# Mixture-of-experts layer: experts in order of their counts, with rooms shrinking from 208 to 160 slots and a packed down product

## The chip, the cores and the metric

One core of a Trainium2 chip runs one inference step of a small hybrid diffusion backbone. The metric is the device time of the whole program in microseconds. All arithmetic is float32; products run as pairs of rounded parts ("high" and "low", type fp32r) of both operands.

## The reference, cut to what matters

Two layers run over 640 tokens (128 context, 512 latent) of 1024 features. Layer 0 has a dense channel mixer. Layer 1 has the routed one, which the change concerns:

```python
def moe_swiglu(h, w_router, w_gu, w_down):
    t = h.reshape(B * L, D)
    logits = (t @ w_router).astype(jnp.float32)
    top_v, top_i = lax.top_k(logits, TOP_K)              # 2 of 8 experts
    top_w = jax.nn.softmax(top_v, axis=-1)
    gates = jnp.einsum('nk,nke->ne', top_w, jax.nn.one_hot(top_i, N_EXPERTS, ...))
    gu = jnp.einsum('nd,edf->enf', t, w_gu)              # 1024 -> 2 x 1408
    g, u = jnp.split(gu, 2, axis=-1)
    eo = jnp.einsum('enf,efd->end', jax.nn.silu(g) * u, w_down)   # 1408 -> 1024
    return jnp.einsum('ne,end->nd', gates, eo)
```

The 640 tokens make 1280 token-expert pairs, 160 per expert on average. The kernel computes each expert only on the tokens that chose it. Everything ahead of this layer (modulation, two attention and convolution mixers, the dense mixer) is left alone by the change.

## The kernel before, in words

**Engines and chunks.** Weights stream in chunks of 128 x 1024 float32 (512 KB). SP sends each chunk into one of six raw buffers (`load`, L576; a chunk is sent once the one six before it has been split). ScalarE rounds it to the high part (`split_hi`, L1313-1319), VectorE subtracts to get the low part (`split_lo`, L1864-1867); there are three slots of split weights, so the split of chunk c + 2 stands in the queues of both engines at item c. TensorE waits on `lo_done` for the chunk it needs.

**One list sets the order.** `main_items` (L86) writes out the routed layer: "idx", five "xt", then per expert two "tr", 22 "gu" and 11 "down" items, the next expert's "tr" standing between its predecessor's "gu" and "down". Every engine walks this list in its own `main_expert` (TensorE L1175, ScalarE L1605, VectorE L2431). The last expert's part also has "turn" items and, for VectorE and ScalarE, the mixing of finished rows ("comb", "gate", "join").

**An expert.** Each of the eight experts gets CAP = 208 slots, as a block of 128 and one of 80 (`ROWS`, L28), and they are taken in the order 0 to 7.
- "tr": the gathered token rows `gx` are transposed (L1204) into `hg`, 208 columns of high and 208 of low part for each of eight blocks of features.
- "gu" (`up_chunk`, L1101): for each block, the high weights meet both parts in one matmul of 416 columns (L1108, L1112) and the low weights meet the high part in one of 208 (L1109, L1111). ScalarE and VectorE add the two halves, apply silu and multiply (L1630 to L1652, L2479 to L2492), and split the result into `ea_hi` (L1645, L1652) and `ea_lo` (`lo_part`, L1870-1872).
- "down" (`down_chunk`, L1115): the activations are the stationary side. For each of the two slot blocks there are three products (high-high, low-high, high-low) of two matmuls of 512 columns, 12 matmuls a chunk. ScalarE copies the first block's output to `ey`, VectorE the second's (L2515); POOL's queue writes them to `y_rows` in HBM (`put_rows`, L1777), and gathers the rows of the expert after the next (`fetch_rows`, L1744).
- The last expert's output stays on chip and is scattered by matmuls (L1095, L1149).

**The way in.** VectorE makes the ranks from two counting matmuls (L2289-2298), the selection matrix of expert 0 (`selection(0)`, L2300), the largest count, and from it the flag `most_ready`. TensorE turns the selection into row numbers ("idx", L1195), POOL gathers the rows of expert 0 (L1753). All engines read the largest count and branch: with every count up to 208 they take the path above, else a general path of four rounds over all experts. Meanwhile TensorE transposes the residual stream ("xt", L1171), ScalarE copies it out (L1638), and behind the fifth copy VectorE computes where each token's rows lie (`places`, L2414). SP sends the first six chunks of expert 0 before the route is known (L694); chunks 0 and 1 are split by the last two steps of the output projection ahead (L1494, L2182). Behind the branch it sends the rest (L714-717).

**Later one-time work.** In expert 6's fifth pair, VectorE builds the selection of expert 7 (`selection(LAST_E)`, L2496); POOL then fetches the finished rows of experts 0 to 5 in ten indirect transfers (`fetch_outputs`, L1784), and those of expert 6 later.

## Time and profile before

| | |
|---|---|
| median of 3 runs | 1947.54 us (1946.64 to 1948.92) |
| profiled execution | span 1944.9 us; the page prints no other time for it |
| routed layer, from its first up matmul to the last down matmul | 1234.0 to 1918.7 us of the span |
| TensorE busy | 1889.4 us, 97% |
| VectorE, ScalarE, POOL busy | 1121.2, 799.7, 139.1 us |
| moved | 283.0 MB read, 12.3 MB written |
| granted TensorE clock | 0.992 of full |

The span goes from the first to the last instruction; the timed value has a little around it. A matmul's printed duration includes its pipeline, so two neighbours overlap: what a matmul costs is the distance between starts, or a run of them divided by its count. The same holds, less so, for VectorE and ScalarE.

### The profile page before, as it was taken

To read this page: it belongs to the slowest core of one execution; us is meant where nothing else is said; L and a number is where in the kernel's file an instruction comes from. 1 tells how busy PE (TensorE), PEld (TensorE's weight loads), DVE (VectorE), ACT (ScalarE), POOL (GpSimd) and SP (SyncE) were. 2 spreads that over 40 slices of the span, in tenths; PEclk is the share of its full clock that TensorE was granted. 3 is DMA by queue.
4 is the path that set the end of the run, shared out by engine and by line. 5 is a ranking of instruction groups with operands and counts; after the bars stand their busy time and mean duration, and the time that the engine had idled before them with its cause. 6 is when DMAs were issued, how large, how long until landed. Compare 5 with 4: busy or idle time off the path is not lost.

```text
span 1944.9 us, 30525 instructions
## 1 busy us (share of the span) xinstructions
PE 1889.4 (97%) x12501; PEld 1727.8 (89%) x12501; DVE 1121.2 (58%) x1796; ACT 799.7 (41%) x1334; POOL 139.1 (7%) x109
## 2 busy tenths in 40 slices
PE   8999999999999999999999899899999999999998
PEld 6999768999999999999997597889898988989886
DVE  2643785543433434447347844667676766768576
ACT  4221364322211222232213643556565655656564
POOL 2000000100000000110000012220000000002211
PEclk8999999999999999999999999999999999999999
DMA  9425100334231432304261021678677776768762
GB/s 353 176 90 217 55 1 22 109 112 177 70 120 44 184 120 68 127 25 194 110 194 33 1 68 64 158 232 247 222 247 229 208 240 203 244 203 311 250 197 71
DMA packets 94068, 291.55 MB, mean 150 GB/s; under 512 B 15348, under 2 KB 23924, under 8 KB 93920
## 3 DMA queue, kind: packets, MB, share of 16 engines
q1 hardware_dynamic: 86784, 271.20, 42.5%
q0 software_dynamic: 7136, 18.30, 2.9%
q8 instruction: 102, 1.67, 0.4%
q14 instruction: 46, 0.38, 0.1%
HBM read 283.02 MB, written 12.28 MB: 152 GB/s over the span
## 4 chain that ended last, share of the span: by engine, by line
PE 91%; DVE 5%; ACT 1%; issue 1%; DMA 1%; SPq 0%; POOL 0%; POOLq 0%; ACTq 0%; DVEq 0%
PE ps L740 47%; PE ps L1119 12%; PE ps L1108 12%; PE ps L1109 6%; PE ps L806 2%; PE ps L935 2%; PE ps L881 2%; PE ps L1112 2%; DVE nbias L2020 1%; PE ps L1111 1%; DVE pr L2037 1%; DMA ada_raw<-ada_w 1%; PE ps L1204 1%; ACT pT L1448 0%; PE ps L942 0%
## 5 line engine op out<-in xcount | busy, mean ns | idle before, releaser
L1867 DVE TENSOR_TENSOR w_lo<-raw,w_hi 128x1024 fp32r<-128x1024 f32 x394 | 482.3, 1226 | 386.8 <-ACT w_hi L1319 378.2
L1319 ACT ACTIVATE w_hi<-raw 128x1024 fp32r<-128x1024 f32 x394 | 414.4, 1053 | 343.3 <-PE ps L740 171.1
L1108 PE MATMUL ps<-hg,w_hi 128*128 128x416 f32 x1232 | 379.2, 365 | 1.0 <-DVE hg L2314 0.8
L740 PE MATMUL ps<-a_hi,w_hi 128*128 128x320 f32 x1472 | 341.5, 313 | 3.4 <-DVE a_lo L1898 3.4
L740 PE MATMUL ps<-a_hi,w_lo 128*128 128x320 f32 x1472 | 336.4, 310 | 0.0
L740 PE MATMUL ps<-a_lo,w_hi 128*128 128x320 f32 x1472 | 333.5, 307 | 0.0
L1109 PE MATMUL ps<-hg,w_lo 128*128 128x208 f32 x1232 | 319.2, 259 | 0.0
L740 PEld LDWEIGHTS ps<-a_hi,w_hi 128*128 128x128 f32 x1472 | 247.0, 188 | 12.3 <-issue 8.1
L740 PEld LDWEIGHTS ps<-a_lo,w_hi 128*128 128x128 f32 x1472 | 248.3, 188 | 0.0
L740 PEld LDWEIGHTS ps<-a_hi,w_lo 128*128 128x128 f32 x1472 | 245.0, 188 | 0.0
L1109 PEld LDWEIGHTS ps<-hg,w_lo 128*128 128x128 f32 x1232 | 234.7, 191 | 0.4
L1108 PEld LDWEIGHTS ps<-hg,w_hi 128*128 128x128 f32 x1232 | 232.0, 188 | 3.3 <-DVE hg L2314 1.0
L1915 DVE TENSOR_REDUCE bcol<-ps 128x2 f32<-128x4 f32 x84 | 13.5, 161 | 185.1 <-PE ps L740 185.1
L1119 PE MATMUL ps<-w_hi,ea_hi 128*128 128x512 f32 (+1 forms) x352 | 111.6, 398 | 2.0 <-DVE w_lo L1867 2.0
L1119 PE MATMUL ps<-w_lo,ea_hi 128*128 128x512 f32 (+1 forms) x352 | 110.9, 396 | 0.0
L1119 PE MATMUL ps<-w_hi,ea_lo 128*128 128x512 f32 (+1 forms) x352 | 110.5, 395 | 0.0
L1119 PEld LDWEIGHTS ps<-w_hi,ea_hi 128*128 128x128 f32 (+1 forms) x352 | 58.7, 169 | 24.4 <-DVE w_lo L1867 2.5
L740 PE MATMUL ps<-act_lo,w_hi 128*128 128x320 f32 x352 | 80.3, 309 | 0.0
L740 PE MATMUL ps<-act_hi,w_hi 128*128 128x320 f32 x352 | 80.2, 309 | 0.0
L740 PE MATMUL ps<-act_hi,w_lo 128*128 128x320 f32 x352 | 80.1, 309 | 0.0
L1119 PEld LDWEIGHTS ps<-w_hi,ea_lo 128*128 128x128 f32 (+1 forms) x352 | 59.6, 169 | 22.8 <-issue 0.4
L1119 PEld LDWEIGHTS ps<-w_lo,ea_hi 128*128 128x128 f32 (+1 forms) x352 | 59.3, 168 | 22.5
(285 smaller groups left out, 2452.0 us busy)
## 6 DMA issues: line engine op xcount, KB each, us to landing
raw<-gu_w SPq DMA_DIRECT2D x220, 512.0 KB, 4.4
raw<-moe_down_w SPq DMA_DIRECT2D x88, 512.0 KB, 4.3
ada_raw<-ada_w SPq DMA_DIRECT2D x21, 2048.0 KB, 8.1
raw<-in_w SPq DMA_DIRECT2D x48, 512.0 KB, 9.8
raw<-down_w SPq DMA_DIRECT2D x22, 512.0 KB, 3.5
raw<-out_w SPq DMA_DIRECT2D x16, 512.0 KB, 3.5
ada_pro<-ada_w SPq DMA_DIRECT2D x2, 2048.0 KB, 19.2
y_rows<-ey POOLq DMA_DIRECT2D x7, 512.0 KB, 4.0
```

Source lines behind the costliest of these rows:

```text
L740: ins = nc.tensor.matmul(out[:, hf, 0:c1 - c0], w, o[:, c0:c1], start=f, stop=e)
L806: ins = nc.tensor.matmul(ps[32 * j:32 * (j + 1), g % 4, 0, 0:QCOLS], cs[:, QUAD * q + k, :], src[:, k, j * QCOLS:(j + 1) * QCOLS], start=f ...
L881: ins = nc.tensor.matmul(score_rows(l, m)[:, c0:c1], qT[rows, h, t * P:(t + 1) * P], kT[rows, h, k0 + c0:k0 + c1], start=True, stop=True)
L935: ins = nc.tensor.matmul(outputs(l)[:, i % 2, :], pT[:, i % 2, j * P:(j + 1) * P], vtok[:, k0 // P + j, h * VH:(h + 1) * VH], start=(j == ...
L1108: nc.tensor.matmul(sums, whi, both, start=(k == 0), stop=False)
L1109: nc.tensor.matmul(out, wlo, hg[:, k, 0, :], start=False, stop=False)
L1111: nc.tensor.matmul(out, wlo, hg[:, k, 0, :], start=False, stop=False)
L1112: ins = nc.tensor.matmul(sums, whi, both, start=False, stop=True)
L1119: ins = nc.tensor.matmul(ps[0:ROWS[st_], (g + st_) % 4, hf, :], a[:, k, st_ * P:st_ * P + ROWS[st_]], w[:, n % SPLIT, hf * 512:(hf + 1) * ...
L1204: ins = nc.tensor.transpose(ps[:, slot, k // 2, at:at + ROWS[st_]], gx[0:ROWS[st_], st_, (4 * i + k) * P:(4 * i + k + 1) * P], idn[0:ROWS[ ...
L1319: nc.scalar.activation(w_hi[:, s, :], raw[:, n % RAW, :], ACT.Copy).then_inc(hi_done, 1)
L1867: nc.vector.tensor_tensor(w_lo[:, s, :], raw[:, n % RAW, :], w_hi[:, s, :].bitcast(F32), ALU.subtract)\
```

## The change

Experts are taken in falling order of their counts. The position in that order, not the expert's number, sets the room: 208, 192, 184, 176, 168, 160, 160, 160 slots. The flag that picks the general path now says whether any count exceeds its room.

```diff
+ROOM = [CAP] + [max(160, 200 - 8 * _j) for _j in range(1, EXPERTS)]
+NROWS = [[P, _n - P] for _n in ROOM]
+BASE, LOWER = 64, 256
...
+                    totals = before[:, TT, :]
+                    link(nc.vector.scalar_tensor_tensor(key, totals, float(EXPERTS), iot[:, 0:EXPERTS],
+                                                        op0=ALU.mult, op1=ALU.subtract))
+                    link(nc.vector.tensor_reduce(top, key, AX, ALU.max))
+                    link(nc.vector.tensor_scalar(first, key, top, None, ALU.is_equal))
```

VectorE's order of work at the way in (`column_of` is a multiply and a reduction; `overflow` five and `expert_order` six small operations on 8 or 64 columns):

```diff
-                    selection(0)
+                    column_of(rcol[:], r, first)
+                    select_ranks()
+                    shifted_rows(7, 4)
+                    overflow()
+                    main_expert(MAIN[:1])
+                    expert_order()
                     link(nc.vector.tensor_scalar(rank[:, :, EXPERTS:], rank[:, :, 0:1], float(CAP), None, ALU.subtract))
-                    link(nc.vector.tensor_reduce(most[:], before[:, TT, :], AX, ALU.max))
-                    nc.vector.tensor_copy(most_i[:], most[:]).then_inc(most_ready, 1)
-                    shifted_rows(7, 4)
-                    main_expert(MAIN[:1])
                     weights_of_experts()
```

SP no longer sends chunks ahead of the branch; each source address comes out of a register, and chunk 2 and its followers wait for the gathered rows of the first expert:

```diff
-                    for c in range(PRELOAD):
-                        load(n + c, source(0, c))
...
                     with sp.Else():
-                        for c in range(PRELOAD, MAIN_N):
-                            if c == 2 * UNIT_CH:
-                                load_rows_of_gates()
-                            load(n + c, source(c // UNIT_CH, c % UNIT_CH))
+                        sp.wait_ge(order_ready, 1)
+                        for e in range(EXPERTS):
+                            which = sp.value_load(order_i[0:1, e:e + 1], min_val=0, max_val=EXPERTS - 1)
+                            for cc in range(UNIT_CH):
+                                if (e, cc) == (0, 2):
+
+                                    sp.wait_ge(gx_in, 16 * ST)
+                                if (e, cc) == (2, 0):
+                                    load_rows_of_gates()
+                                load(n + e * UNIT_CH + cc, source_of(which, cc))
```

The splits of chunks 0 and 1 move from the output projection behind the third and fifth stream copy (ScalarE; VectorE likewise), and `places()` moves from behind the fifth to behind the first:

```diff
                 for c in range(OUT_CH):
-                    split_hi(n0 + c + 2, q0 + c)
+                    if l == 0 or c < OUT_CH - 2:
+                        split_hi(n0 + c + 2, q0 + c)
...
+                                if i in (2, 4) and part is MAIN:
+                                    split_hi(n0 + i // 2 - 1, q0)
```

In "tr", "gu" and the activation steps, 208 is replaced by the room of the position (on ScalarE and VectorE too):

```diff
-                                ins = up_chunk(n0 + c, ps[:, slot, 0, 0:CAP], ps[:, slot, 0, 0:2 * CAP])
+                                ins = up_chunk(n0 + c, ps[:, slot, 0, 0:ROOM[e]], ps[:, slot, 0, 0:2 * ROOM[e]],
+                                               gathered_rows(e))
```

From the second position on, the slots above 128 (at most 64) lie with their high part in columns 0 to 63 of one 128-column stationary block and their low part in columns 64 to 127. The first position keeps `down_chunk`.

```diff
+                    def down_lower(n, g, k):
+
+                        for a, w in ((0, w_hi), (1, w_hi), (0, w_lo)):
+                            for hf in range(2):
+                                ins = nc.tensor.matmul(ps[:, g % 4, hf, :], ea[:, k, LOWER * a:LOWER * a + P],
+                                                       w[:, n % SPLIT, hf * 512:(hf + 1) * 512],
+                                                       start=(k == 0 and a == 0 and w is w_hi),
+                                                       stop=(k == FB - 1 and w is w_lo))
+                        return ins
+
+                    def down_upper(n, g, k):
+
+                        for w in (w_hi, w_lo):
+                            for hf in range(2):
+                                ins = nc.tensor.matmul(ps[:, (g + 1) % 4, hf, :], ea[:, k, P:2 * P],
+                                                       w[:, n % SPLIT, hf * 512:(hf + 1) * 512],
+                                                       start=(k == 0 and w is w_hi), stop=(k == FB - 1 and w is w_lo))
+                        return ins
...
+                    def expert_lo(e, f, some, done):
...
+                        nc.vector.tensor_tensor(ea[:, f, P + BASE:BASE + some], full[:, P:some], hi[:, P:some].bitcast(F32),
+                                                ALU.subtract)
+                        nc.vector.tensor_tensor(ea[:, f, LOWER:LOWER + P], full[:, 0:P], hi[:, 0:P].bitcast(F32),
+                                                ALU.subtract).then_inc(alo_done, 1)
...
-                                    nc.vector.tensor_copy(ey[rows, 1, :].rearrange("p (a b) -> p a b", a=2),
-                                                          ps[rows, (g0 + g + 1) % 4]).then_inc(ey_ready, 1)
...
+                                        link(nc.vector.tensor_copy(rest, upper[BASE:BASE + NROWS[e][1]]))
+                                        nc.vector.tensor_tensor(rest, rest, upper[top_rows], ALU.add).then_inc(ey_ready, 1)
```

At the last position, the last chunk's packed product comes first; ScalarE copies its lower half and VectorE adds the other half ahead of `last_outputs`. The last expert's selection and gates are picked out of the tables by its place in the order:

```diff
-                                    selection(LAST_E)
+                                    last_expert()
...
+                    def last_expert():
+
+                        one = perm[:, LAST_E, :]
+                        column_of(glast_f, gates[:], one)
+                        link(nc.vector.tensor_copy(glast[:, :, 0], glast_f))
+                        link(nc.vector.tensor_tensor(glast[:, :, 1], glast_f, glast[:, :, 0].bitcast(F32), ALU.subtract))
+                        column_of(rcol[:], rank[:, :, 0:EXPERTS], one)
+                        select_ranks()
```

The numbers of the slots in `places` use the position instead of the expert (four more small operations).

## Rows read from the trace of the kernel before

**Rows 1.** The page: busy time, share of the span and instructions of each engine.
```profile
PE 1889.4 (97%) x12501; PEld 1727.8 (89%) x12501; DVE 1121.2 (58%) x1796; ACT 799.7 (41%) x1334; POOL 139.1 (7%) x109
```
**Rows 2.** Stretches: length, busy PE, PEld, DVE, ACT, POOL; clock; DMA share; GB/s.
```profile
1319.30:1372.00 52.70, 52.70 (x354) 52.54 (x353) 41.46 (x63) 34.63 (x65) 3.69 (x4) 1.00 0.81 247
...
1785.00:1797.00 12.00, 12.00 (x81) 11.96 (x81) 9.20 (x15) 8.05 (x16) 1.67 (x2) 1.00 0.96 374
```
**Rows 3.** The chain of work that ended last: start us, us, what.
```profile
1144.06 44.19 PE ps L740 x300
...
1288.55 30.66 PE ps L1119 x132
1372.03 1.47 PE ps L1204 x16
...
1711.85 1.47 PE ps L1204 x16
...
1797.20 1.47 PE ps L1204 x16
```
**Rows 4.** Groups of instructions from 1150 us on: busy us, mean ns, idle before.
```profile
L1867 DVE TENSOR_TENSOR w_lo<-raw,w_hi 128x1024 fp32r<-128x1024 f32 x269 | 329.2, 1226 | 174.5 <-ACT w_hi L1319 168.8
...
L2479 DVE TENSOR_TENSOR st<-st,ps 128x208 f32<-128x208 f32 x88 | 32.7, 371 | 18.4 <-ACT st L1630 18.3
...
L2515 DVE COPY ey<-ps 80x1024 f32<-80x1024 f32 x7 | 8.5, 1221 | 2.8 <-PE ps L1119 2.8
```
**Rows 5.** Timeline, TensorE in an up chunk: start us, us, engine, line, operation.
```profile
1256.00 0.37 PE L1108 MATMUL ps<-hg,w_hi 128*128 128x416 f32 x1
...
1256.20 0.26 PE L1109 MATMUL ps<-hg,w_lo 128*128 128x208 f32 x1
...
1256.30 0.37 PE L1108 MATMUL ps<-hg,w_hi 128*128 128x416 f32 x1
```
**Rows 6.** Timeline, weight loads of the two-column matmuls of the "turn" items.
```profile
1844.02 0.64 PEld L1134 LDWEIGHTS ps<-grouped,sel 128*128 128x128 f32 x5
...
1847.55 0.47 PEld L1134 LDWEIGHTS ps<-grouped,sel 128*80 128x80 f32 x5
```
**Rows 7.** Timeline, VectorE in expert 6 just behind the selection of expert 7.
```profile
1773.30 1.23 DVE L1867 TENSOR_TENSOR w_lo<-raw,w_hi 128x1024 fp32r<-128x1024 f32 x1
...
1777.18 1.23 DVE L1867 TENSOR_TENSOR w_lo<-raw,w_hi 128x1024 fp32r<-128x1024 f32 x1
```
**Rows 8.** Timeline, the one-time work of the last two experts; idle time in brackets.
```profile
1769.24 1.27 DVE L2306 TENSOR_SCALAR sel<-iot,rank 128x208 fp32r<-128x208 f32 x5
...
1891.81 1.06 PE L1119 MATMUL ps<-w_hi,ea_hi 128*128 128x512 f32 x2 [2.01 <-DVE w_lo L1867]
...
1918.72 1.41 DVE L2349 SCALAR_TENSOR_TENSOR ey<-ps,gslot,x 128x512 f32<-128x512 f32 x2 [1.14 <-PE ps L1119]
```
**Rows 9.** Timeline, the way into the routed layer, one engine after the other.
```profile
1216.49 1.05 PE L1195 MATMUL ps<-tok,sel 128*128 128x2 f32 x10
...
1215.40 1.27 DVE L2250 SCALAR_TENSOR_TENSOR yab<-ps,rms,pr 128x1024 f32<-128x1024 f32 x1
...
1223.98 2.92 ACT L1638 ACTIVATE x_tok<-ps 128x1024 f32<-128x1024 f32 x3 [4.03 <-issue]
...
1230.85 1.62 ACT L1555 ACTIVATE hg<-ps 128x832 fp32r<-128x832 f32 x2 [1.81 <-PE ps L1204]
...
1221.85 36.97 SPq L581 DMA_DIRECT2D raw<-gu_w  x12
```
**Rows 10.** Loads: the page's landing times, those from 1140 to 1260 us, and issue ns.
```profile
raw<-gu_w SPq DMA_DIRECT2D x220, 512.0 KB, 4.4
...
raw<-gu_w SPq DMA_DIRECT2D x18, 512.0 KB, 8.4
...
L581 SPq DMA_DIRECT2D raw<-gu_w x220: 327/328/3296, 329.6 to 1865.2; - x110
```

More of the change, by code:

```diff
@@ L409, in hybrid_step, with gathered_rows @@
         ht_lo = a_lo[:].rearrange("p a b -> p (a b)").rearrange("p (t d) -> p t d", t=TT)
+        spare = cs[:].rearrange("p k c -> p (k c)")
+        key, first, pos, over = (spare[:, EXPERTS * _i:EXPERTS * (_i + 1)] for _i in range(4))
+        top, glast_f, posit = spare[:, 32:33], spare[:, 40:40 + TT], spare[:, 48:48 + 2 * TT]
+        posit = posit.rearrange("p (t o) -> p t o", o=2)
+        pairs = spare[:, 64:64 + EXPERTS * EXPERTS].rearrange("p (j e) -> p j e", j=EXPERTS)
+        perm = spare[:, 128:128 + EXPERTS * EXPERTS].rearrange("p (j e) -> p j e", j=EXPERTS)
+        picked = spare[:, 192:192 + TT * EXPERTS].rearrange("p (t e) -> p t e", t=TT)
+        ea_two = ea[:].rearrange("p f (a c) -> p f a c", a=2)
+        def gathered_rows(e):
+            return hg[:].rearrange("p k a c -> p (k a c)")[:, 0:KB * 2 * ROOM[e]]\
+                .rearrange("p (k a c) -> p k a c", k=KB, a=2)
         rstd = ss[:].rearrange("p (a b) -> p a b", a=2)
@@ L702, in _ @@
                     sp.wait_ge(most_ready, 1)
-                    with sp.If(sp.value_load(most_i[0:1, 0:1], min_val=0, max_val=T) > CAP):
+                    with sp.If(sp.value_load(most_i[0:1, 0:1], min_val=0, max_val=EXPERTS) > 0):
+                        for c in range(PRELOAD):
+                            load(n + c, source(0, c))
                         load_rows_of_gates()
@@ L1712, in _ @@
                     act.wait_ge(most_ready, 1)
-                    with act.If(act.value_load(most_i[0:1, 0:1], min_val=0, max_val=T) > CAP):
+                    with act.If(act.value_load(most_i[0:1, 0:1], min_val=0, max_val=EXPERTS) > 0):
                         main_expert(MAIN[:len(START)])
+                        for c in range(2):
+                            split_hi(n0 + c, q0)
                         for t in range(TT):
@@ L2309, in selection, with column_of @@
                         ins.then_inc(sel_ready, 1)
-                    def gathered_lo(slot, i, done):
+                    def selection(e, count):
+                        nc.vector.tensor_copy(rcol[:], rank[:, :, e]).then_inc(rcol_set, 1)
+                        dve.wait_ge(rcol_set, count)
+                        select_ranks()
+                    def column_of(dst, table, one):
+                        link(nc.vector.tensor_tensor(picked, table, one.unsqueeze(1).broadcast_to([P, TT, EXPERTS]),
+                                                     ALU.mult))
+                        link(nc.vector.tensor_reduce(dst, picked, AX, ALU.add))
@@ new lines, in overflow @@
+                    def overflow():
+                        link(nc.vector.tensor_tensor(pairs, totals.unsqueeze(1).broadcast_to([P, EXPERTS, EXPERTS]),
+                                                     room[:].unsqueeze(2).broadcast_to([P, EXPERTS, EXPERTS]), ALU.is_gt))
+                        link(nc.vector.tensor_reduce(over, pairs, AX, ALU.add))
+                        link(nc.vector.tensor_tensor(over, over, iot[:, 0:EXPERTS], ALU.subtract))
+                        link(nc.vector.tensor_reduce(most[:], over, AX, ALU.max))
+                        nc.vector.tensor_copy(most_i[:], most[:]).then_inc(most_ready, 1)
```

205 lines of the change are left out of this document (132 added, 73 removed).

## The prediction

> **What bounds the kernel now.** I read the busy table first: TensorE is busy for 97% of the span [rows 1], so only its time, and what it waits for, can move the end. Then the table by stretches: the up phase of one expert (two projections, 22 weight chunks) keeps TensorE at 100% and at the full clock, and the DMA engines at 0.81 [rows 2]. The chain gives the pace: 132 down matmuls in 30.66 us, 232 ns each; the 22 up chunks lie between 1288.55 + 30.66 = 1319.21 and 1372.03, which is 52.8 us or 2.40 us a chunk, eight pairs of 300 ns; 300 matmuls of 320 columns elsewhere take 147 ns each [rows 3]. One expert takes (1711.85 - 1372.03) / 4 = 84.95 us, eight of them some 680 [rows 3]. Of the side engines VectorE is nearest: 1.23 us for each chunk's low part, and four operations of 0.37 us for each pair of chunks [rows 4].
>
> **How much a pair shrinks.** A pair is a "high" matmul of 2 x 208 columns and a "low" one of 208, starting 0.20 and 0.10 us apart [rows 5]. From 320 to 512 columns the time grows by (232 - 147) / 192 = 0.443 ns a column [rows 3]; on that line 416 columns cost 190 ns and 208 cost 98, together 288, while the pair takes 300. So with 190 for the high one, the low one takes 110. Its neighbour shows why: during the low matmul the 128-column weights of the next high one are loaded. Where matmuls have only two moving columns, such loads follow each other by (0.64 - 0.19) / 4 = 112 ns with 128 weight columns and by (0.47 - 0.15) / 4 = 80 ns with 80 [rows 6]. I read the low matmul as waiting for that load already. Fewer slots then shorten the high matmul alone: 2 x 0.443 = 0.89 ns a slot and pair.
> Two rules of the Trainium skill pull apart here, both on the page TensorE: Matmul & The Clock Gate. The section "Wait — 56ns, not 53.3ns?" has warm matmuls start N / 2.4 + 2.5 ns apart; by it alone the low matmul would fall from 89 to 69 ns and the up phases would give 60 us. The section "LDWEIGHTS (loading the stationary operand)" has a load of P columns take P / 1.2 ns, 107 for 128, which forbids just that. The 112 ns of the bare loads side with the second.
>
> **The sum: gains.** Rooms are 208, 192, 184, 176, 168, 160, 160, 160: 256 slots fewer over eight experts. Up: 176 pairs an expert x 256 x 0.89 ns = 40 us. Down: for the seven experts behind the first, 12 matmuls a chunk become 10 (six for the slots under 128, four for the packed block): 7 x 11 x 2 = 154 x 232 ns = 36 us. The transposes of the gathered rows (1.47 us for 16 [rows 3]) lose at most 0.3 us each expert; I take none. Gains 76 us.
>
> **What the side engines do then.** A pair of chunks in a room of 160 lasts 2 x 8 x (300 - 48 x 0.89) = 4.12 us on TensorE. VectorE, when it is behind and waits for nobody, needs 3.88 us for its share of such a pair at 208 slots (its chunk splits at 1773.30 and 1777.18) [rows 7]. Narrower operations take off 4 x 48 x (1226 - 371) / 816 = 0.2 us [rows 4]; the packed low part is two operations for one, bounded by nothing and another 0.37, taken as 0.1. So 3.8 against 4.1: it stays covered, but its spare time per pair falls from 0.9 us to 0.3. ScalarE's share shrinks and adds nothing in the loop. Where VectorE gets extra work, TensorE now waits sooner:
> - Each expert's output of the packed block is a copy and an add instead of one copy of 1.22 us [rows 4]: VectorE reaches the third chunk's split 1.2 us later, about 2 x 1.22 + 1.23 + links = 3.9 us into the up phase, where that chunk is due at 4.1. Covered; 0.
> - Expert position 6 (the last but one) builds the last one's selection inside its up phase: 1.27 us for five compares [rows 8] and six operations on single columns, under 0.2 us each; TensorE waited (1797.20 - 1711.85) - 84.95 = 0.4 us for these [rows 3]. Six more of 0.2 us come, and the lead over TensorE shrinks by two chunk times of 0.34. I take 2 us more, between 1 and 3.5.
> - The last expert's up phase has three row mixings of 1.2 us each on VectorE; the pair then asks 3.8 + 1.2 = 5.0 against 4.12: 3 x 0.9 less a lead of about 1.3, 1.3 us. Behind it TensorE waited 2.01 us for a split whose chain (last product, table load, mixing, split) does not depend on it [rows 8]; the two down chunks that cover it are 4 x 232 ns shorter: 0.9 us more.
> - At the end, VectorE waited 1.14 us for the last down matmul before it scaled the outputs [rows 8]. The last three down chunks are now 3 x 0.46 = 1.4 us shorter, and the add of the packed block (1.2 us) is put before the scaling: -1.14 + 1.4 + 1.2 = 1.5 us on the tail.
> Together 5.7 us.
>
> **The start of the routed layer.** Before, six chunks were loaded and two split long before the route was known, under the output projection; the new order of experts is known only behind the counts. VectorE now does, ahead of the branch flag (till now written just before the row shift that starts at 1215.40 [rows 9]), three operations for the largest expert, two for its column, five for the overflow test, and the row shift of 1.3 us that stood behind it: 10 x 0.2 + 1.3 = 3.3 less one rank operation of 0.2, so the flag comes at about 1218.5. The index matmuls start at 1216.49 behind filler matmuls of TensorE's own [rows 9], so the 1.0 us ahead of the selection is hidden there; without the fillers it would be on the path. The index results are read about 0.8 us later; six operations for the order (1.3 us) stand ahead of the gate weights that ScalarE waits for before it branches, so its first stream copy moves from 1223.98 to about 1226.2. Behind its third and fifth copies it now makes two splits (2 x 1.05 us), where before the gathered rows arrived last; places() moves behind the first copy and is off the path. Sum: 2.2 + 2.1, less the 1.8 that ScalarE idled for the gathered rows at 1230.85 [rows 9]: 2.5 us. SP issued its first chunk after the branch at 1221.85 [rows 9]; with the flag 3.2 us later but only 1.5 us behind its own last store before, that becomes about 1223.5, plus reading the order; loads land in 4.4 us [rows 10], at best at 1228, at worst (8.4 us, the median of the loads in this stretch [rows 10]) after 1232, where ScalarE wants them at 1229.5. The third chunk is sent behind the gathered rows and has two chunks' time left. I take 3 us, between 2 and 8. The two splits taken out of the projection stood beside its matmuls and give nothing back.
>
> **Loads.** Every weight load gets a source address out of a register, and SP reads one number per expert. No row shows such a load; the nearest are 0.33 us median and 3.3 us at most per issue [rows 10]. SP needs one per 2.07 us in the shortest rooms and runs up to five chunks ahead: I take 0. The data: 512 KB per 2.07 us is 253 GB/s beside row traffic, where stretches that are full moved 374 [rows 2]. Only the early fetch of finished rows fills the engines; it may delay weights by 0 to 4 us; I take 0.5.
>
> **Sum:** 40 + 36 - 5.7 - 3 - 0.5 = 67 us off the profiled span of 1944.9, which gives 1878. The page prints no other time for that execution; the median of the runs, 1947.5, is 2.6 above the span, and 67 off it is 1880.5; I say 1881. The sum's own bounds: gains 74 to 78, costs 5 to 20, so 1873 to 1893.
>
> **Rivals.**
> - *The low matmul shrinks too* (12%). For it: the pair's 300 ns differ from the line's 288 by 12 only. Against: 112 ns between bare loads. Then 176 x 256 x 0.443 = 20 us more: 1861, less where VectorE (3.8) then bounds the pairs of the short rooms (3.84), so about 1863. It is the outcome of the first of the two rules of the Trainium skill named above (TensorE: Matmul & The Clock Gate).
> - *Weights come late* (14%): the chunks are requested at the same lead of six buffers but used 16% faster; full stretches stood at a share of 0.96 already [rows 2]. If the fetches and the start each cost what they can, 4 + 5 us, and the small stalls come at their upper bounds, 1893 or a few more.
> - *SP becomes the bound, and the kernel slower* (2%): a load with a register address would have to cost SP over 84.9 / 33 = 2.57 us; at the longest issue of the trace, 3.3 us, 231 loads give 231 x 0.73 = 168 us more than now, 2115. The median of 0.33 speaks against it.
> - *The shrunk path is not taken* (under 1%): where counts exceed rooms, all engines take the general path of four rounds, well over a millisecond slower. The reference's routing of the given inputs has the sorted counts 205, 179, 176, 150, 148, 148, 138, 136; all fit.
> My forecast has the other 71%. The range of 8 in 10, 1864 to 1895, takes in the first rival's upper part, the bounds above and most of the second. A measurement of this kernel tells 0.2% (4 us) from no change: faster 0.97, same 0.01, slower 0.02.
>
> **What the profile after would show.** The high matmuls of short rooms 147 ns and the low ones still 0.10 to 0.11 us apart, the last rooms' up phase 45.5 us; if it is 42.5, the first rival holds. Ten matmuls a down chunk, 2.32 us. VectorE without "idle" before its splits in the short rooms, yet no TensorE wait beside those named. The first up matmul near 1237. A wait of TensorE on w_lo that goes back to raw and DMA would show the second rival; SP issues longer than 2 us the third.

## The result, and the profile after

| | before | after |
|---|---|---|
| median | 1947.09 us (1944.95 to 1948.92, 4 runs) | 1916.29 us (1912.51 to 1921.1, 4 runs) |
| profiled execution | span 1944.9 us | 1912.51 us, span 1910.7 us |
| granted TensorE clock | 0.992 | 0.985 |

The ratio is 0.9842, with a 95% interval from 0.9828 to 0.9857. The change gains 31 us where 67 were forecast; the time lies outside the range of 1864 to 1895.

TensorE is still what bounds the kernel, as in [rows 1]; the page of the changed kernel:

```profile
PE 1844.9 (97%) x12347; PEld 1690.1 (88%) x12347; DVE 1115.5 (58%) x1907; ACT 790.8 (41%) x1335; POOL 142.7 (7%) x109
```

**What came as forecast.** The up phases of the short rooms, in the table by stretches and in the timeline of one chunk (columns as in [rows 2] and [rows 5]):

```profile
1326.50:1376.70 50.20, 50.20 (x354) 50.17 (x352) 40.51 (x72) 34.18 (x65) 3.63 (x4) 1.00 0.83 253
1638.10:1683.60 45.50, 45.50 (x354) 45.38 (x352) 39.01 (x74) 33.10 (x65) 3.18 (x4) 1.00 0.89 285
```

```profile
1659.85 0.35 PE L1144 MATMUL ps<-hg,w_hi 128*128 128x320 f32 x1
1660.04 0.24 PE L1145 MATMUL ps<-hg,w_lo 128*128 128x160 f32 x1
1660.11 0.34 PE L1144 MATMUL ps<-hg,w_hi 128*128 128x320 f32 x1
```

A room of 160 takes 45.5 us, the forecast's number, with the clock at 1.00 and TensorE never idle. But the pair is not divided as I had said: the high matmul still takes 0.19 us to the next start, and the low one 0.07. I come back to this below.

**What did not.** The chain of waits, at the transposes of the gathered rows and in the tail (start us, us, what; the transposes answer to L1204 in [rows 3]):

```profile
1292.13 3.53 PE ps L1259 x16
...
1762.55 3.32 PE ps L1259 x16
...
1878.46 4.94 PE ps L1204 x12
1883.40 13.32 PE ps L1131 x24
```

The 16 transposes took 1.47 us before; from the second position on they take 3.3 to 3.5. And the last 24 scatter matmuls take 13.32 us, 555 ns each. The stretches of the tail, of the changed kernel (columns as in [rows 2]):

```profile
1880.00:1884.00 4.00, 4.00 (x10) 1.67 (x10) 0.16 (x1) 1.97 (x4) 0.00 (x0) 0.99 0.00 0
1884.00:1888.00 4.00, 4.00 (x8) 2.00 (x8) 0.44 (x1) 1.85 (x4) 0.00 (x0) 0.50 0.00 2
...
1896.00:1900.00 4.00, 4.00 (x18) 3.35 (x18) 2.68 (x4) 1.45 (x3) 2.16 (x2) 0.50 0.00 0
```

and a stretch of the same work in the kernel before:

```profile
1926.00:1930.00 4.00, 4.00 (x19) 3.25 (x18) 1.94 (x4) 3.66 (x8) 0.00 (x0) 1.00 0.00 0
```

The busy share of TensorE is full in all four lines; only the number of matmuls (19 in 4 us before, 10 and then 8 after) and the granted clock tell. The clock stands at 0.50, the lower of its two levels (1.2 GHz), from 1884 to 1901 us, some 17 us. The timelines show the pace just ahead of the fall: TensorE's matmuls, then its weight loads, with their idle time in brackets.

```profile
1881.62 0.93 PE L1204 MATMUL ps<-ey_hi,selT 128*128 128x512 f32 x2
1882.48 0.93 PE L1204 MATMUL ps<-ey_lo,selT 128*128 128x512 f32 x2
```

```profile
1881.62 0.19 PEld L1204 LDWEIGHTS ps<-ey_hi,selT 128*128 128x128 f32 x1 [0.25 <-issue]
1882.05 0.18 PEld L1204 LDWEIGHTS ps<-ey_hi,selT 32*128 32x128 f32 x1 [0.25 <-issue]
```

Two matmuls take 0.86 us, 430 ns each, where before they took 230. The loads alternate between 128 and 32 rows (`32*128`), and each begins together with its own matmul and not under the one ahead.

**The account of the profiled executions**, from first start to first start of each phase in the two traces, set beside the terms of the prediction:

| term | forecast us | measured us |
|---|---|---|
| up phases, narrower matmuls | +40 | +38.4 |
| down phases, 10 matmuls for 12 | +36 | +34.8 |
| transposes, positions 1 to 7 | 0 | -14.4 |
| selection in position 6 | -2 | -3.8 |
| last expert, row mixings | -1.3 | -2.6 |
| last expert, splits in the down phase | -0.9 | -1.1 |
| tail, behind the last down matmul | -1.5 | -12.0 |
| way in, up to the first up matmul | -3 | -4.7 |
| loads | -0.5 | 0 |
| first up phase, two chunks at half clock | 0 | -1.7 |
| everything ahead of the route | 0 | +1.4 |
| sum | +67 | +34.3 |

1944.9 - 34.3 = 1910.6, the span after. (The row on the selection holds 1.6 us of lower clock, that on the row mixings 1.7 us of a wait for gathered rows; both are taken up below.) Two rows, the transposes and the tail, make 25 of the 33 us that are missing, and they have one thing in common: tiles of 64 rows or fewer.

### The profile page after: what moved, and what is told of

Read it like the earlier page. It is cut to its first block, busy times and chain, and to the rows that moved or that the text cites. A ratio compares the mean times of both kernels' runs of the same rounds, so it can differ in the third digit from the quotient of the medians.

```text
span 1910.7 us, 30889 instructions
## 1 busy us (share of the span) xinstructions
PE 1844.9 (97%) x12347; PEld 1690.1 (88%) x12347; DVE 1115.5 (58%) x1907; ACT 790.8 (41%) x1335; POOL 142.7 (7%) x109
## 4 chain that ended last, share of the span: by engine, by line
PE 88%; DVE 5%; issue 2%; ACT 2%; DMA 1%; POOL 0%; SPq 0%; ACTq 0%; DVEq 0%; POOLq 0%
PE ps L776 48%; PE ps L1144 11%; PE ps L1167 6%; PE ps L1145 5%; PE ps L1177 4%; PE ps L842 2%; PE ps L971 2%; PE ps L917 2%; PE ps L1155 2%; PE ps L1148 2%; PE ps L1259 1%; DVE nbias L2099 1%; PE ps L1147 1%; DVE pr L2116 1%; PE ps L1131 1%
## 5 line engine op out<-in xcount | busy, mean ns | idle before, releaser
L1144 PE MATMUL ps<-hg,w_hi 128*128 128x320 f32 (+5 forms) x1232 | 348.0, 352 | 6.3 <-DVE w_lo L1943 4.0
L1145 PE MATMUL ps<-hg,w_lo 128*128 128x160 f32 (+5 forms) x1232 | 301.5, 245 | 0.0
L1991 DVE TENSOR_REDUCE bcol<-ps 128x2 f32<-128x4 f32 x84 | 13.5, 160 | 184.9 <-PE ps L776 184.8
L1167 PE MATMUL ps<-w_hi,ea 128*128 128x512 f32 x308 | 85.9, 401 | 3.6 <-DVE w_lo L1943 3.6
L917 PE MATMUL ps<-kT,qT 64*128 64x512 f32 (+2 forms) x288 | 63.4, 486 | 11.9 <-ACT pr L1501 11.9
L1594 ACT ACTIVATE act_hi<-tt 128x640 fp32r<-128x640 f32 x22 | 16.3, 740 | 140.9 <-DVE tt L2000 140.9
L1501 ACT ACTIVATE pr<-ps,nbias 128x768 f32<-128x768 f32 (+1 forms) x80 | 63.5, 794 | 26.6 <-DVE nbias L2099 15.3
L1167 PEld LDWEIGHTS ps<-w_hi,ea 128*128 128x128 f32 x308 | 57.6, 189 | 17.4 <-DVE w_lo L1943 4.3
```

Of the source, the lines that this page charges most:

```text
L917: ins = nc.tensor.matmul(score_rows(l, m)[:, c0:c1], qT[rows, h, t * P:(t + 1) * P], kT[rows, h, k0 + c0:k0 + c1], start=True, stop=True)
L1144: nc.tensor.matmul(sums, whi, both, start=(k == 0), stop=False)
L1145: nc.tensor.matmul(out, wlo, rows_[:, k, 0, :], start=False, stop=False)
L1167: ins = nc.tensor.matmul(ps[:, g % 4, hf, :], ea[:, k, LOWER * a:LOWER * a + P], w[:, n % SPLIT, hf * 512:(hf + 1) * 512], start=(k == 0 a ...
L1501: nc.scalar.activation(pr[:, i % 2, s, 0:nk], score_rows(l, m)[:, 0:nk], ACT.Exp, bias=nbias[:, m % 4:m % 4 + 1], accum_out=rsum[:, STEPS[ ...
```

## The experiments

The median of a kernel stands against the changed kernel's 1916.3 us unless another is named; each set had its own runs of the kernel before, whose medians lay between 1947.3 and 1948.5.

**tr80: the transposes on 80 rows.** Rooms, order and packing stay.

```diff
-    at, some = (k % 2) * ROOM[e] + st_ * P, NROWS[e][st_]
+    at, some = (k % 2) * ROOM[e] + st_ * P, (P, 80)[st_]
```

> The changed kernel with the second-block transposes of positions 1 to 7 widened to 80 rows (and 80 output columns), as position 0 has them; nothing else. Theory A (a stationary tile of 64 rows or fewer, taken in turn with one of 128, costs far more than one of 80): the 16 transposes at positions 1 to 7 go from 3.3 to 3.5 us back to about 1.5 us, the time falls by 7 x 1.9 = 13 us, to about 1903. Rival B (they are slow because of the place of the rooms in PSUM, the clock, or the late gathered rows): 3.3 us stay, no change within 2 us, 1916.

Measured: 1898.44 us (1896.42 to 1898.78), 18 us less. The chain of waits:

```profile
1292.30 1.47 PE ps L1259 x16
```

More rows and more columns, and less than half of the time. Rival B is out: neither the place in PSUM nor the rooms nor the gathered rows matter. By the chain 13.5 of the 18 us are the transposes; the rest is inside the spread of the changed kernel, whose reason appears under before64.

**tr_order: the same small tiles, grouped.** Four transposes of 128 rows, then the four small ones.

```diff
-    for k in range(4):
-        for st_ in range(ST):
+    for st_ in range(ST):
+        for k in range(4):
```

> The changed kernel with the same 16 transposes, but in each group of eight first the four of 128 rows, then the four of the rest (64 to 32 rows): the small tiles stay, the changes between the two sizes fall from 15 to 3. Theory A in the form that the change of size costs: 16 transposes in about 2.0 us, the time 7 x 1.4 = 10 us lower, about 1906. Theory A in the form that each small tile is slow by itself: 3.3 us stay, 1916.

Measured: 1902.85 us (1895.42 to 1904.03), 13 us less. Its chain, and its weight loads in the timeline:

```profile
1291.87 1.80 PE ps L1259 x16
```

```profile
1293.21 0.32 PEld L1259 LDWEIGHTS ps<-idn,gx 64*128 64x128 f32 x4 [0.17 <-issue]
```

Four loads of 64 rows follow each other within 0.32 us; a small tile is not slow. Only the load behind a change of size waits, 0.17 us here. The 16 transposes take 3.53 us with 15 changes and 1.80 us with 3: the price is (3.53 - 1.80) / 12 = 0.14 us a change between such short matmuls.

**before64: the other direction, on the kernel before.** Nothing of the change is in it. Slots 192 to 207 of six experts are not filled.

```diff
-    at = (k % 2) * CAP + st_ * P
+    at, some = (k % 2) * CAP + st_ * P, (P, 80 if e in (0, 5) else 64)[st_]
```

> The kernel before, with the second-block transposes of six experts (all but 0 and 5) on 64 rows instead of 80; no other change (slots 192 to 207 of those experts are not filled; none of them has so many tokens). Theory A: 16 transposes from 1.43 to 3.6 us at each of the six, 13 us slower than before, about 1960. If the slow transposes needed something else of the change (rooms, order, packing): 1947 to 1949.

Measured: 1967.57 us (1960.77 to 1971.59), ratio 1.01 (1.0072 to 1.0129), 20 us slower than before. The chain at the second expert, and a stretch of it:

```profile
1286.86 3.54 PE ps L1204 x16
1290.40 32.40 PE ps L1119 x132
```

```profile
1291.00:1292.00 1.00, 1.00 (x4) 0.81 (x3) 0.67 (x1) 1.00 (x2) 0.00 (x0) 0.50 0.00 0
```

The slow transposes come back without rooms, order or packing: 6 x 2.07 = 12.4 us. And there is a second cost that I had not expected: behind four of the six the down phase takes 32.4 us where it took 30.7 [rows 3], because the granted clock falls to 0.50 just behind the transposes. That is 4 x 1.74 = 7.0 us more, together 19.4. (From first start to first start the same time divides into 6 x 2.2 us for the transposes and 4 x 1.6 us for the clock.) Whether the clock falls differs from one place and run to the next. In the profiled run of the changed kernel it fell behind none of the seven; in those of late_each and tail_order behind two, in that of low_wide behind four. The four times of each kernel with the slow transposes scatter by 8 to 11 us, those of tr80, rows72 and rows80 by 2 to 5. That the clock is the reason is likely and not shown: the times of tr_order and tail_order2, whose transposes are not slow, scatter by 9 and 10 us.

**tail80: the last expert's scatter on 80 rows.** Rows 32 to 79 carry a zero gate.

```diff
-    rows = slice(0, NROWS[LAST_E][st_])
+    rows = slice(0, ROWS[st_])
...
-    scatter(lg + t, t, hf, 1, NROWS[LAST_E]).then_inc(mm_done, 1)
+    scatter(lg + t, t, hf, 1, ROWS).then_inc(mm_done, 1)
...
```

> The changed kernel with the last expert's scatter matmuls, output scaling and its high and low parts on 80 rows instead of 32 in the second block (rows 32 to 79 carry a zero gate). Theory A: scatter matmuls 230 ns apart as before the change instead of 430 at the full clock. Theory C (the fall of the granted clock to half in the tail follows from that slower pace): the clock stays at 1.0 to the end, and from the last down matmul to the end it takes 28 us instead of 38.4: 10 to 11 us lower, about 1906. Rival D (the clock falls for another reason, such as the wait ahead of the tail): the pace is mended only at the full clock, 40 matmuls lose 0.1 to 0.2 us each for half of them, 3 to 4 us lower, about 1912, and the clock row still shows 0.5.

Measured: 1901.85 us (1900.53 to 1911.59), 14 us less. Timeline and stretch of the tail:

```profile
1880.15 0.40 PE L1131 MATMUL ps<-ey_hi,selT 80*128 80x512 f32 x1
1880.38 0.40 PE L1131 MATMUL ps<-ey_lo,selT 80*128 80x512 f32 x1
```

```profile
1882.00:1886.00 4.00, 3.85 (x19) 2.87 (x18) 2.82 (x5) 3.69 (x6) 0.86 (x1) 1.00 0.02 4
```

230 ns a matmul, the clock at 1.00 to the end of the scatter. From the start of the last down matmul to the end it takes 28.3 us; in the changed kernel it was 38.6, before 26.6. The 1.7 us that remain over before are close to the term of 1.5 that I had for the later add. Rival D does not hold in this run, since the clock no longer falls. All profiled runs agree: in the scatter of the six kernels with 32 rows in turn with 128 (the changed one, tr80, tr_order, low_wide, late_each, tail_order) the clock was at 0.50 for 17 to 20 us, in that of the five others with 72 or 80 rows (rows72, rows80, unpack, nogx and this one) it never fell; in split_sel it fell for a short time behind a wait. Three of the four executions of tail80 lie within 2.5 us; the fourth, of which there is no trace, took 1911.6 us at a mean granted clock of 0.985 where the others had 0.989 and 0.990. The slow transposes are still in this kernel, so it may have lost the clock there.

**rows72 and rows80: both repairs together**, once with 72 rows and once with 80. In rows72 the transposes of the first position have 72 rows too, so its slots 200 to 207 are not filled, although its expert has 205 tokens: the kernel leaves five rows out.

> Both repairs together on the changed kernel, at the least row count that could tell: the second-block transposes of positions 1 to 7 and the last expert's second-block scatter on 72 rows. If the boundary lies between 64 and 72 rows: 16 transposes in 1.5 us, scatter 235 ns apart, clock 1.0 in the tail, 14 + 11 = 25 us below the changed kernel, about 1888 to 1891. If what counts is how far the rows are from 128 (80 is near enough, 72 less so): transposes between 1.5 and 3.3 us, about 1900. Against: 1914 if 72 behaves as 64.

> As rows72, with 80 rows. The gains of the two single repairs (14 to 18 us and 11 to 14 us) should add up, since one is spread over the experts and the other in the tail: 1887 to 1890, and the same as rows72 within 2 us. If they were one effect of the clock they would not add up: 1898.

Measured: 1887.75 us (1886.39 to 1889.98) and 1885.40 us (1882.42 to 1887.68); for rows80 the ratio to before is 0.9675 (0.9659 to 0.9692). With 72 rows the 16 transposes (timeline) are as fast as with 80, 1.38 us to the next start:

```profile
1375.04 1.58 PE L1259 MATMUL ps<-idn,gx 128*128 128x128 f32 x16
1376.42 0.47 PE L1167 MATMUL ps<-w_hi,ea 128*128 128x512 f32 x1
```

The step lies between 64 and 72 rows (3.6 us at 64), and below it little changes: 3.4 us at 32. The two repairs add up, 18 + 14 = 32 against 31. With 80 rows the kernel is 62 us faster than the one before and 31 us faster than the changed one.

**tail_order and tail_order2: small tiles in the tail, grouped.** What was still open was whether the clock falls for the slow pace or for the 32-row matmuls themselves. tail_order regroups token tiles 2 to 4 of the changed kernel; tail_order2 regroups all five and has the transposes of tr80.

```diff
+    for st_ in range(ST):
+        rows = slice(0, NROWS[LAST_E][st_])
+        for h in range(2):
+            for part in (ey_hi, ey_lo):
+                ins = nc.tensor.matmul(ps[:, (lg + t) % 4, h, :], ...
```

> The changed kernel (32 rows kept), but for token tiles 2, 3 and 4 the scatter takes the four 128-row matmuls of both halves first, then the four of 32 rows: 6 changes of tile size instead of 12. If the changes of size alone set the pace, a tile's eight matmuls take some 2.3 us at the full clock instead of 3.4, and if the slow pace is what brings the clock down, it stays up longer: 4 to 8 us less, 1908 to 1912. If the clock falls for the 32-row matmuls themselves or had fallen before: still 0.5 in those stretches, 1 to 3 us less, 1914.

> tr80 (transposes on 80 rows, 1898.4 us) with the last expert's scatter still on 32 rows in the second block, but regrouped for all five token tiles: four matmuls of 128 rows, then four of 32 rows, so 9 changes of tile size in the tail's 40 scatter matmuls where there were 19. If the slow pace (430 ns) is what brings the clock down: the matmuls go at 230 to 300 ns, the clock stays at 1.0, and the tail is within 2 us of that with 80 rows: 1886 to 1889. If matmuls of 32 rows bring the clock down by themselves: 0.5 again in the tail, 1893 or more.

Measured: 1904.82 us (1902.31 to 1910.81) and 1890.69 us (1887.08 to 1897.17). In the profiled run of tail_order the clock fell before the regrouped tiles began, so this trace decides nothing about the clock:

```profile
1880.00:1884.00 4.00, 4.00 (x8) 1.91 (x8) 0.16 (x1) 2.08 (x4) 0.00 (x0) 0.59 0.00 0
```

Still the median is 11.5 us under that of the changed kernel, more than the 4 to 8 expected. The three executions without a trace took 1902 to 1905 us at a mean granted clock of 0.988 to 0.990, the profiled one 1910.8 us at 0.984. In them the clock may have held in the tail; no trace shows it.

tail_order2, timeline and stretch:

```profile
1866.04 0.40 PE L1386 MATMUL ps<-ey_lo,selT 128*128 128x512 f32 x1
1866.36 0.49 PE L1386 MATMUL ps<-ey_hi,selT 32*128 32x512 f32 x1
1866.70 0.39 PE L1386 MATMUL ps<-ey_lo,selT 32*128 32x512 f32 x1
1866.93 0.39 PE L1386 MATMUL ps<-ey_hi,selT 32*128 32x512 f32 x1
```

```profile
1865.00:1869.00 4.00, 4.00 (x16) 2.35 (x15) 1.54 (x3) 3.83 (x8) 0.00 (x0) 1.00 0.01 2
```

Matmuls of 32 rows follow each other in 230 ns like those of 128. At a change the two neighbours take 0.32 and 0.34 us: 0.2 us a change. The first sixteen scatter matmuls of the changed kernel change size every time, 232 + 200 = 430 ns, which is its pace; the later 24 change every second time. (My expectations counted the changes of the tail too low, and took 430 ns for all of them.) With the changes thinned out the clock stayed at 1.00 although half of the matmuls still use 32 rows, so matmuls of 32 rows alone do not bring it down, and the slow pace remains as the cause. That is shown for one profiled run, the fastest of the four. The median of 1890.69 us lies between what I expected for the pace (1886 to 1889) and for the 32 rows (1893 or more), and the times go up to 1897.17 us at a mean granted clock of 0.982, so in some executions the clock may still have fallen.

**low_wide: does the low matmul shrink?** The low matmul reads 208 columns in every room; the columns beyond the room meet the low part of the rows, a product that the kernel otherwise leaves out.

```diff
-    nc.tensor.matmul(out, wlo, rows_[:, k, 0, :], start=False, stop=False)
+    nc.tensor.matmul(out, wlo, both[:, 0:CAP], start=False, stop=False)
```

> The changed kernel with every low-part matmul of the up phases on 208 moving columns again, in rooms of 160 too (the columns beyond the room meet the low part of the rows, a product that the kernel otherwise leaves out). My step (the low matmul takes what the load of the next weights takes, 110 ns, whatever its columns): no change within 3 us, 1914 to 1917, up phases at 45.5 us for a room of 160. The rival of the prediction (the low matmul shrinks with its columns): 176 x 256 x 0.443 ns = 20 us slower, 1935, up phases 49.2 us.

Measured: 1917.75 us (1913.92 to 1923.42), no change. Timeline, a room of 160:

```profile
1668.35 0.33 PE L1144 MATMUL ps<-hg,w_hi 128*128 128x320 f32 x1
1668.52 0.26 PE L1145 MATMUL ps<-hg,w_lo 128*128 128x208 f32 x1
1668.61 0.33 PE L1144 MATMUL ps<-hg,w_hi 128*128 128x320 f32 x1
```

The up phase of this room is 45.8 us, with 160 columns 45.5; over positions 1 to 5 the up phases take 240.0 us together, and 240.3 in the changed kernel. The wider low matmul takes 0.09 us instead of 0.07, and the high one behind it 0.17 instead of 0.19: the pair is 0.26 us either way. So the columns of the low matmul are free, as I had claimed. The wait for the next weights shows in the gap behind the high matmul, not in that of the low one, as I had written it.

**unpack: the down product unpacked at positions 1 to 6**, on rows80.

```diff
-    if e == 0:
-        ins = down_chunk(n0 + c, g0 + g, i)
+    if e < LAST_E:
+        ins = down_chunk(n0 + c, g0 + g, i, e if e else None)
...
```

> rows80 with the down product of positions 1 to 6 unpacked: 12 matmuls a chunk, the second block's with 64 to 32 stationary columns, one copy of its output instead of a copy and an add. By my term: 66 chunks x 2 x 232 ns = 31 us slower, 1916, 30.7 us for each down phase, and nothing in the up phases. If 64 stationary columns and fewer broke the overlap of loads as 64 rows and fewer do, each chunk would lose 0.3 us or more beside that: 1936 or more. If the copy and the add of the packed block cost something in the following up phase, that phase gets shorter than 50.3, 49.1, 48.5, 46.8, 45.5 us.

Measured: 1914.85 us (1913.59 to 1917.87), 29.5 us over rows80. The chain at the second position, and a piece of its timeline:

```profile
1375.21 30.69 PE ps L1156 x132
```

```profile
1376.49 1.09 PE L1156 MATMUL ps<-w_hi,ea 128*64 128x512 f32 x4
1377.41 0.63 PE L1156 MATMUL ps<-w_lo,ea 128*64 128x512 f32 x2
```

30.69 / 132 = 232 ns again. The packing is worth what I said, and nothing of it is given back in the up phases but possibly in position 6 (47.8 us against 48.1 and 49.6 in two runs with the packing, which differ by the clock). A stationary block of 64, 40 or 32 *columns* in turn with one of 128 costs nothing (`128*64` is rows by columns); only rows do.

**late_each: a semaphore for each tile's late rows.** In the profile of the changed kernel ScalarE stood 1.80 us in the last up phase:

```profile
1833.13 1.16 ACT L1690 ACTIVATE yab<-yab,g 128x1024 f32<-128x1024 f32 x1 [1.80 <-DMA yab<-y_rows,late]
```

```diff
-    if i == 0:
-        act.wait_ge(late_rows, 16 * 2 * TT)
+    act.wait_ge(late_rows[i], 16 * 2)
...
-    if 2 * t + o == 5:
+    if each is None and 2 * t + o == 5:
         pool.wait_ge(done, 16 * (2 * t + o))
```

The second part means that POOL no longer waits for the first five transfers before it issues the sixth.

> The changed kernel with one semaphore for each token tile's late rows, so that the row mixing of tile 0 waits for its own two transfers and not for all ten. Theory E (ScalarE's wait for the last of the ten late transfers, in the middle of the last up phase, holds back the splits behind it): the wait of 1.8 us at 1833 goes, TensorE's waits for w_lo in the last expert fall from some 7 us to 2 or 3, the time 4 us lower, about 1912. Rival F (VectorE's three mixings alone are too much for the shorter chunks): the waits stay within 1 us, about 1915.

Measured: 1915.35 us (1910.99 to 1918.88), no change. TensorE's waits from 1700 us on, of the changed kernel and of late_each (line, releaser: us in all, times, longest):

```profile
PE ps L1144 <- DVE w_lo L1943: 4.0, 2, 2.3
PE ps L1167 <- DVE w_lo L1943: 3.6, 2, 3.1
```

```profile
PE ps L1167 <- DVE w_lo L1943: 3.6, 2, 3.1
PE ps L1144 <- DVE w_lo L1943: 2.3, 1, 2.3
```

TensorE's wait of 1.7 us is gone, but the semaphores did not remove it. Without POOL's wait the tenth transfer was issued at 1818.3 us instead of 1826.6 and had landed by 1824.7, long before the first row mixing at 1833.3. And the wait comes and goes in kernels that still wait for all ten transfers: it is absent in tr80, tr_order, tail80, tail_order and nogx, and there in rows72, rows80, low_wide, unpack, split_sel and tail_order2, where TensorE stands for 0.7 to 1.6 us. So Theory E explains up to 1.7 us of an execution. What it is worth in the median is not told apart from nothing.

**split_sel: VectorE's block in position 6 spread over three pairs**, on rows80.

```diff
-    if f == 4 and e == LAST_E - 1:
-        last_expert()
+    if e == LAST_E - 1 and f in (1, 2, 4):
+        (last_gates, last_ranks, None, select_ranks)[f - 1]()
```

> rows80 with the last expert's gates picked in the second pair of position 6, its rank column in the third, and only the five compares (1.27 us) left in the fifth. Theory G (the stall of 4.2 us in position 6's up phase is VectorE's block of ten operations in one place): the phase falls from 49.65 to about 48 us, the time by 1.5 us, to 1884. Rival (VectorE has no slack in any pair of these rooms, so the work costs the same wherever it stands): 49.6 us, no change.

Measured: 1884.63 us (1882.07 to 1886.12) against 1885.40 for rows80: not told apart. The phase itself fell from 49.65 to 47.1 us, more than expected. But in the profiled run the tail took it back, with 30.7 us from the start of the last down matmul to the end where rows80 has 28.3: TensorE waited 2.0 us for `ey_hi` where it had waited 0.5, then the clock fell. Its waits, and the stretch behind:

```profile
PE ps L1144 <- DVE w_lo L1943: 2.3, 2, 1.3
PE ps L1204 <- ACT ey_hi L1631: 2.0, 2, 1.8
```

```profile
1858.00:1862.00 4.00, 3.85 (x8) 2.12 (x9) 3.79 (x6) 1.72 (x3) 0.00 (x0) 0.57 0.00 0
```

VectorE is busy 3.8 us of 4 there, without a pause between the last row mixings and the scaling of the outputs. I read it so that its work does not move with TensorE's, which comes earlier and waits longer; that reading is from one run.

**nogx: SP's wait for the gathered rows taken out**, on rows80.

```diff
-    if (e, cc) == (0, 2):
-        sp.wait_ge(gx_in, 16 * ST)
```

> rows80 without SP's wait for the gathered rows ahead of chunk 2. If the wait delays the third chunk's split: up phase 0 shorter by up to 1 us, 1884. If without it the weight loads take the transfer engines from the gathered rows: the first up matmul 1 to 3 us later, 1887. I expect the first up matmul no earlier and the difference inside 2 us.

Measured: 1887.97 us (1886.42 to 1888.97), 2.6 us over rows80 across two sets of runs (ratios 0.9691 and 0.9675, whose intervals overlap); first index matmul to first up matmul 21.8 us against 22.1. The kernel without the wait is the slower one, by a little more than the 2 us I allowed for, so the wait costs nothing.

## Why the prediction was wrong

**The steps that failed.** "The transposes of the gathered rows (1.47 us for 16) lose at most 0.3 us each expert; I take none." They cost 2.0 us each, 14.4 in all. I had priced the narrower second block by its columns, and a fall from 80 rows to 64, 56, 48, 40 and 32 as if it could only help. The same omission is in the tail: "-1.14 + 1.4 + 1.2 = 1.5 us" speaks of when the scatter begins, and leaves its own matmuls at their old pace. They went from 80 rows to 32, the first sixteen at 430 ns instead of 230, and behind that pace the clock fell: 12.0 us where I had 1.5. By the prices of the runs the changes of size are some 5 us of it (15 x 0.2 + 12 x 0.2, an estimate), the lower clock the rest. None of the rows I had read shows a tile under 80 rows beside one of 128, so the term had to be bounded from both sides: 0 was one end, and a load that lies under no matmul was the other.

I had overlooked that the trace of the kernel before holds the price. In the attention ahead of the routed layer, matmuls of 64 rows (L881) follow some of 128 (timeline, the first matmuls behind such a change and their weight loads):

```profile
1044.80 0.70 PE L881 MATMUL ps<-kT,qT 64*128 64x512 f32 x2
1044.80 0.30 PEld L881 LDWEIGHTS ps<-kT,qT 64*128 64x128 f32 x4 [0.19 <-issue]
```

The load waits 0.19 us and begins together with its matmul. The 128-row matmul ahead of it takes 0.24 us to the next start, its equals further ahead 0.15. Where the 128-row ones come back, at 1041.10 us, the first of them takes 0.25 us for 0.15, and the 64-row one ahead of it about 0.1 us too long as well: 0.2 us a change, the price that tail_order2 shows.

The Trainium skill has the rule I passed over: on the page TensorEngine Tiling (Array Packing), section "Key Properties", a change of the tiling mode, and not just of the tile, drains TensorE. The same page of the Trainium skill lists 64 and 32 rows as such modes (section "Available Configurations"), and 64 and 32 columns as well. For rows this case's runs agree: 0.2 us a change, nothing inside a group, and the step between 64 and 72. For columns they show no such cost: unpack has 232 ns a matmul where blocks of 64 to 32 columns stand in turn with 128. Whether those loads put TensorE into another mode at all, no run shows.

**The clock as a second price.** The forecast took all durations at the full clock. Where TensorE's pace fell, by changes of size or by a wait, the granted clock fell to 0.50 behind it in some executions and held in others. In position 6 (changed kernel):

```profile
1738.00:1742.00 4.00, 1.91 (x9) 1.91 (x10) 3.60 (x10) 1.70 (x4) 2.20 (x2) 0.82 0.08 18
1742.00:1746.00 4.00, 4.00 (x25) 4.00 (x25) 2.71 (x5) 1.70 (x5) 3.37 (x3) 0.75 1.01 369
```

TensorE stands for 2.1 of the first 4 us, and then the clock is at half for a part. The stall of 2.3 us is the one I priced at 2, and 1.6 us of lower clock come on top. In nogx, with the same stall, the clock held, and the phase took 48.07 us instead of 49.65:

```profile
1726.00:1730.00 4.00, 1.68 (x13) 1.45 (x12) 3.54 (x13) 0.70 (x4) 1.28 (x1) 1.00 0.22 86
```

In the first up phase it is the same: 54.6 or 53.05 us, depending on the run.

**What held.**
- The up phases: 38.4 us for 40. The price of 0.89 ns a slot and pair gives 7.5 us for a room of 160 and 7.3 were measured; low_wide shows that the low matmul's columns are free, so the first rival (it shrinks too, 12%) is out. Where the wait sits within a pair I had wrong.
- The down phases: 34.8 us for 36, confirmed by unpack.
- VectorE's cover in the short rooms: no TensorE wait in any room of 168 or 160 but those named, and the packed block's copy and add are hidden.
- The way in. Its steps, in the timeline of the changed kernel (VectorE's flag, ScalarE's stream copies and its split, SP's loads, VectorE's split, the first up matmul), are to be read 1.4 us later against [rows 9], because this execution was that much ahead:

```profile
1216.93 0.15 DVE L2410 CAST most_i<-most 128x1 int32<-128x1 f32 x1
...
1225.01 1.94 ACT L1703 ACTIVATE x_tok<-ps 128x1024 f32<-128x1024 f32 x2 [4.09 <-PE ps L1226]
1228.63 1.02 ACT L1703 ACTIVATE x_tok<-ps 128x1024 f32<-128x1024 f32 x1 [1.69 <-PE ps L1226]
...
1221.53 17.62 SPq L604 DMA_DIRECT2D raw<-gu_w  x9
...
1233.95 1.23 DVE L1943 TENSOR_TENSOR w_lo<-raw,w_hi 128x1024 fp32r<-128x1024 f32 x1 [2.10 <-ACT w_hi L1383]
...
1237.34 0.46 PE L1144 MATMUL ps<-hg,w_hi 128*128 128x416 f32 x1 [2.26 <-DVE hg L2450]
```

The flag comes at 1217.1 + 1.4 = 1218.5 (forecast 1218.5), the first copy at 1226.4 (1226.2), SP's first chunk at 1222.9 (1223.5). What I did not have is ScalarE's wait of 1.69 us for TensorE's third stream transpose. So 4.7 us instead of 3, within the 2 to 8 that I allowed.
- Loads and SP: no TensorE wait goes back to a load of weights, so the second rival (14%) is out; SP's loads out of a register never held it up, so the third is out as well. The general path was not taken.

With both repairs the measured 1885.4 us lies 4.4 above the forecast. The shortfalls in the table that the repairs do not touch (the up and down phases 2.8, the selection 1.8, the first up phase 1.7, the way in 1.7, the row mixings 1.3) more than cover it. The mechanism of the gains was right; what was wrong is that a smaller tile was taken to cost at most what the larger one did.

Three figures of the working are off, and nothing hangs on them. The 60 us given for the Trainium skill's rule were worked out with the rows' 0.443 ns a column and not with that rule's own figure. The first rival's pair of 3.84 us is 16 x (300 - 3 x 48 x 0.443) ns = 3.78. And the lower bound of 1873 is 1947.5 - 78 + 5 = 1874.5.

## What to carry to other kernels

When a change makes a tile smaller, price each matmul that uses it on all three of its sizes (contraction rows, stationary columns, moving columns), and look whether it crosses 64 rows next to matmuls of 128: either pad it (80 rows cost nothing here) or group equal sizes. And a stretch in which TensorE is "busy" all the time can still run at half its pace; count matmuls in equal stretches and read the granted clock beside it, since a stretch of slow pace can cost as much again through the clock.

## What the runs showed of the hardware that was not expected

- Matmuls with 64 contraction rows or fewer in turn with 128-row ones: each change keeps the next weight load from going under the matmul ahead. It costs 0.2 us between matmuls of 512 columns (tail_order2) and 0.14 between transposes (tr_order). 72 and 80 rows in turn with 128 cost nothing, nor do 64 or 32 stationary columns, nor small tiles among themselves (0.32 us for four loads of 64 rows).
- The granted clock fell to 0.50 behind the slow transposes (3.5 us for 16), in four of six places of one execution, and cost 1.6 us each; behind scatter matmuls 430 ns apart it fell in all six kernels profiled and stayed down for 17 to 20 us. With the same 32 rows and fewer changes it stayed at 1.00 in the one run profiled.
- A pair of a 320-column matmul and a small one under it, each with a new 128-column stationary block, takes 0.26 us whether the small one has 160 or 208 columns.
